# Two mixer stacks with feed-forward layers on one core: spreads by transposition, and another order around the layer norm in the first stack's output stage

## Chip, core and metric

The kernel runs on one core of a Trainium2 chip. The metric is the device time in microseconds of one execution. Before the change the median of three runs is 1272.53 us (1272.1 to 1272.92).

## What is computed

An input of 256 positions by 1024 channels, in float32, goes through two stacks. **Stack 1** is two mixer layers and a final RMS norm; **stack 2** is two layers of feed-forward, mixer, feed-forward, and a last norm. The change touches the mixer layers of stack 1 and the row scale of every norm. Cut to that:

```python
def hybrid_layer(x, ...):                       # stack 1, twice
    h = rmsnorm(x, norm_g)
    proj = h @ w_in                             # 14 pieces of 256 columns in the kernel
    y_a = silu(layernorm(depthwise_conv(a_u * sigmoid(a_v), conv_a_w) + conv_a_b, ln_g, ln_b)) * silu(a_z)
    y_b = b_b * depthwise_conv3(b_c * b_x) * silu(b_z)
    y_c = window_attention(c_q, c_k, c_v, sink) * silu(c_z)
    y_d = neighbourhood_attention(d_q, d_k, d_v, rpb) * silu(d_z)
    return x + concat(y_a, y_b, y_c, y_d) @ w_out
```

The convolution is 31 taps wide. Both attentions have 4 heads of 64 channels and divide by the softmax sum.

## The kernel before, in words

**Precision.** Every large product is made of three: each float32 operand is split into a high part in fp32r, made on ScalarE (`round_hi`, L512), and the remainder, made on VectorE (`split_lo`, L936). TensorE runs high by high, high by low and low by high (`product`, L1659 to L1661). The norm's factor 1/rms is applied after the projection, so TensorE can start before it is known: `spread_rows` (L1724) turns the 128 x 2 values of `rstd` into a row for all partitions, by a plain float32 matmul whose stationary operand is the value broadcast to 128 columns and whose moving operand is the identity; ScalarE copies the result to `row_scale`, by which VectorE's `copy_out` (L989) multiplies each projection on its way out of PSUM. This is done eight times, once for each norm ahead of a projection.

**A mixer layer of stack 1.** Weights arrive in slots of 1 MB through a ring of three. Slots 0 to 13 are the projections in the order of `ORDER_1`, slots 14 to 17 the output matrix in the order `WOUT_1` (c, d, b, a). Every engine has its own hand-written program, a loop over the slots, and semaphores with running counts join them. TensorE's slot i of `project` needs the split weights (`lo_ready`) and a free PSUM bank (`copy_out` of slot i - 2). The attention is done in four units (window attention for the two halves of the queries, then neighbourhood attention for the two). Unit u has its scores after slot u + 7, its softmax on VectorE and ScalarE, its transposition in the midst of slot u + 9 (`turn_probs`, L1800), and its values after slot u + 9 (`values`, L1811), into the PSUM tile `mix`. The exponentials aren't normalized. Instead `finish` on VectorE takes the reciprocal of the four row sums (`row_inv`, 128 x 4, L1016), one slot after the scores, and TensorE's `spread_inverse` (L1820) spreads them over the channels into the PSUM tile `aux`, by four float32 matmuls of 64 columns each, after the values. `gated_y` on VectorE (L1144, L1148) multiplies `aux`, the gate and `mix`; the values of unit u + 1 may be written only after this has read `mix`.

**VectorE's order in a slot** is `copy_out`, `finish`, the softmax's bias and maximum (`soft`, L999, L1004), `gated_y`, some convolution taps (L1129, `DVE_TAPS_AT`), `split_lo`, and a gate product (L1210). The last four taps are in slot 12, behind `gated_y` of the last unit, and then `conv_part` goes up. GpSimd adds the products of the other taps and then the two partial sums (L1582), which raises `conv_ready`.

**The output stage** of stack 1 (slots 14 to 17). Within slot 14 TensorE transposes the convolution to rows of positions (`conv_to_tm`, L1902), VectorE takes mean and variance (L1171, L1172) after `copy_out` of slot 13, GpSimd the inverse root (L1529), VectorE normalizes (L1195), TensorE turns it back within slot 15 (`ln_to_fm`, L1911), VectorE applies gain and bias (L1228), ScalarE makes the tanh of it (L710), and VectorE forms and splits the branch (L1237, L1238, L943, L944). That raises `ya_ready`, for which slot 17 waits; slot 16 waits for the short convolution's branch (`yb_ready`).

Of the kernel before, what the change touches and what calls it, by code (L numbers as in the profile page):

```python
# [11 lines left out]
ACT = mybir.ActivationFunctionType  # L12
# [3 lines left out]
P = 128  # L16
# [65 lines left out]
TURN_AT = 7  # L82
ROT_AT = 4
# [81 lines left out]
def stacks_kernel(nc, a, out):  # L165

    with ExitStack() as ctx:
# [22 lines left out]
        part_sum = sb("part_sum", [P, S])  # L190
        tmp = sb("tmp", [P, 2 * S])
# [120 lines left out]
        ln_ready = sem("ln_ready")  # L312
# [181 lines left out]
        def _(act):  # L494
# [178 lines left out]
            for l in range(DEPTH):  # L673
# [35 lines left out]
                act.wait_ge(ln_ready, l + 1)  # L709
# [207 lines left out]
        def _(dve):  # L917
# [93 lines left out]
            def finish(un, u, has_sink):  # L1011
                c = 4 * (u % 2)
                dve.wait_ge(probs_exp, un + u + 1)
                if has_sink:
                    link(v.tensor_tensor(row_sum[:, c:c + 4], row_sum[:, c:c + 4], sink_e, ALU.add))
                link(v.reciprocal(row_inv[:, c:c + 4], row_sum[:, c:c + 4]))  # L1016
                dve.sem_inc(inv_ready, 1)
# [92 lines left out]
            for l in range(DEPTH):  # L1110
# [43 lines left out]
                for i, name in enumerate(ORDER_1):  # L1154
                    if i == 0:
                        dve.wait_ge(rb_ready, l + 1)
                    if name != "d_v":
                        copy_out(base, i, name, l * NPROJ + i)
                    if i == 4:
                        rotate(step_aux(), proj[:, ix["c_q"], :], cst[:, C_COS:C_COS + S], cst[:, C_SIN:C_SIN + S],  # L1160
                               2, proj[:, ix["c_q"], :])
# [5 lines left out]
                    if i == 13:  # L1167
                        n = step_aux()
                        dve.wait_ge(aux_written, n + 1)
                        for t in range(NT):  # L1170
                            link(v.bn_stats(bn_raw[:, t, :], aux[:, t * S:(t + 1) * S]))  # L1171
                            link(v.bn_aggr(bn[:, t, :], bn_raw[:, t, :]))  # L1172
                        v.tensor_copy(ln_rstd[:], bn[:, :, 1]).then_inc(ho_ready, 1)
# [13 lines left out]
                    if i in DVE_TAPS_AT:  # L1187
                        done = sum(n for at, n in DVE_TAPS_AT.items() if at < i)
                        taps(done, done + DVE_TAPS_AT[i])
                        if done + DVE_TAPS_AT[i] == DVE_TAPS:  # L1190
                            dve.sem_inc(conv_part, 1)
# [8 lines left out]
                    if name in ("a_v", "c_z", "d_z", "b_z", "a_z"):  # L1200
# [24 lines left out]
                n = step_aux()  # L1225
                dve.wait_ge(aux_written, n + 1)
                for c in range(2):
                    ins = v.tensor_scalar(conv_acc[:, c], aux[:, c * S:(c + 1) * S], parA_all[:, l, A_LG + c:A_LG + c + 1],  # L1228
                                          parA_all[:, l, A_LB + c:A_LB + c + 1], ALU.mult, ALU.add)
                    ins.then_inc(aux_read if c else ln_half, 1)  # L1230
                dve.wait_ge(aux_read, n + 2)
                dve.wait_ge(ln_half, l + 1)
                dve.sem_inc(ln_ready, 1)
# [420 lines left out]
        def _(pe):  # L1654
# [64 lines left out]
            def spread_rows(n):  # L1719

                pe.wait_ge(rstd_ready, rms_count(n) * 2 + 2)
                root = rstd_2 if n == DEPTH else rstd
                for t in range(NT):
                    ins = t_.matmul(big[:, 0, t * P:(t + 1) * P], root[:, t:t + 1].to_broadcast([P, P]), ident,  # L1724
                                    start=True, stop=True, skip_group_check=True)
                ins.then_inc(rb_written, 1)
# [88 lines left out]
            def spread_inverse(n, u, order=HORDER):  # L1815
                pe.wait_ge(inv_ready, n + 1)
                for c in range(2):
                    for low in range(2):
                        at = 4 * (u % 2) + order[2 * c + low]
                        ins = t_.matmul(aux[low * HD:(low + 1) * HD, c * P:(c + 1) * P],  # L1820
                                        row_inv[:, at:at + 1].to_broadcast([P, HD]), ident, start=True, stop=True,
                                        skip_group_check=True)
                ins.then_inc(aux_written, 1)
# [15 lines left out]
            for l in range(DEPTH):  # L1839
# [9 lines left out]
                for i, name in enumerate(ORDER_1):  # L1849
                    kind = "TM" if name == "d_v" else "FM"  # L1850

                    def turn_unit():
                        turn_probs(l * 4 + i - SC_1 - 2, i - SC_1 - 2)

                    if i >= 2:
                        between = {TURN_AT: turn_unit} if 0 <= i - SC_1 - 2 < 4 else {}
# [36 lines left out]
                    if 0 <= u - 2 < 4:  # L1893
                        aux_free()
                        spread_inverse(l * 4 + u - 2, u - 2, PLAIN if u - 2 < 2 else HORDER)
                def conv_to_tm():
                    aux_free()
                    pe.wait_ge(conv_ready, l + 1)
                    for t in range(NT):
                        for c in range(2):  # L1900
                            at = t * S + c * P
                            ins = t_.transpose(aux[:, at:at + P], conv_acc[:, c, t * P:(t + 1) * P], ident)  # L1902
                    ins.then_inc(aux_written, 1)

# [9 lines left out]
                for j, grp in enumerate(WOUT_1):  # L1914
# [4 lines left out]
                           {0: {1: conv_to_tm}, 1: {1: ln_to_fm}, 3: {3: lambda: turn_x(l + 1, 0)}}.get(j))  # L1919
# [214 lines left out]
```

## Time and profile before

| | |
|---|---|
| median of three runs | 1272.53 us |
| the profiled execution | 1271.64 us, its span 1269.8 us |
| TensorE matmul busy | 1260.5 us, 99% of the span |
| VectorE busy | 986.7 us, 78% |
| ScalarE busy | 697.5 us, 55% |
| GpSimd busy | 270.0 us, 21% |
| granted TensorE clock over the span | 0.999 of full |

The 1.8 us between the span and the time lie outside of what the profile records. A matmul's recorded duration includes the way through the pipeline, so consecutive ones overlap: the interval between two starts is what one costs, and the busy share can't show short stalls. The chain of waits gives such intervals as its steps. Stack 1 takes the first 257 us, with the two units of layers at 18 to 135 us and 141 to 257 us. Stack 2 is the rest.

### The profile page before, as it was taken

The page shows a single profiled execution, that of the slowest core. Times are in us where ns is not written, and L with a number is a line of the kernel's source. Part 1 is how long each engine was busy: PE and PEld are TensorE (multiplying, and loading weights), DVE is VectorE, ACT ScalarE, POOL GpSimd, SP SyncE. Part 2 cuts the span into 40 slices and gives each one's busy share as a digit, 9 for nine tenths or more (in the row PEclk, how much of TensorE's full clock was granted, in tenths as well). Part 3 has the DMA queues.
Part 4 walks back from the last instruction along what each step waited for, and adds up shares of the span by engine and source line. Part 5 has one row for each costly group of instructions (what it writes and reads, how often), then busy time and mean ns, then how long its engine had stood idle before and what let it go on. Part 6 is the DMA issues. An engine that isn't in the chain of part 4 may idle for free.

```text
span 1269.8 us, 21116 instructions
## 1 busy us (share of the span) xinstructions
PE 1260.5 (99%) x7986; PEld 1124.0 (89%) x7986; DVE 986.7 (78%) x1187; ACT 697.5 (55%) x929; POOL 270.0 (21%) x258
## 2 busy tenths in 40 slices
PE   9999999999999999999999999999999999999998
PEld 8998999888888899988888888888889998888886
DVE  6999789898767679868767778767676986877676
ACT  6674567465444586836444455444458673644444
POOL 2763275283000113201000009100011420100000
PEclk9999999999999999999999999999999999999999
DMA  9854654647666554346666655766654535566661
GB/s 281 257 183 166 202 147 150 180 146 222 198 189 187 156 165 144 128 141 185 196 184 185 198 166 176 214 182 190 198 161 138 166 134 150 177 189 197 193 186 52
DMA packets 281359, 224.02 MB, mean 176 GB/s; under 512 B 25996, under 2 KB 264234, under 8 KB 281288
## 3 DMA queue, kind: packets, MB, share of 16 engines
q1 hardware_dynamic: 279144, 220.23, 57.5%
q10 hardware_dynamic: 2032, 2.67, 0.6%
q8 instruction: 47, 0.77, 0.2%
q14 instruction: 24, 0.20, 0.0%
q0 software_dynamic: 112, 0.15, 0.0%
HBM read 221.85 MB, written 3.14 MB: 177 GB/s over the span
## 4 chain that ended last, share of the span: by engine, by line
PE 90%; DVE 6%; ACT 2%; issue 2%; DMA 0%; POOLq 0%; SPq 0%; DVEq 0%; POOL 0%; ACTq 0%
PE wide L1692 26%; PE wide L1695 13%; PE big L1659 9%; PE big L1660 9%; PE big L1661 8%; PE wide L1659 6%; PE wide L1660 6%; PE wide L1661 6%; DVE w_lo L936 2%; PE wide L1811 1%; PE big L1716 1%; PE big L1800 1%; PE big L1786 1%; DVE work L1345 1%; PE wide L1981 1%
## 5 line engine op out<-in xcount | busy, mean ns | idle before, releaser
L936 DVE TENSOR_TENSOR w_lo<-w_raw,w_hi 128x2048 fp32r<-128x2048 f32 x203 | 475.0, 2342 | 94.5 <-ACT w_hi L512 90.2
L512 ACT ACTIVATE w_hi<-w_raw 128x2048 fp32r<-128x2048 f32 x204 | 389.6, 1911 | 165.0 <-PE big L1661 125.2
L1692 PE MATMUL wide<-h_both,w_hi 128*128 128x512 f32 x1408 | 356.7, 393 | 0.0
L1692 PEld LDWEIGHTS wide<-h_both,w_hi 128*128 128x128 f32 x1408 | 254.6, 189 | 48.5 <-DVE h_both L951 2.0
L1659 PE MATMUL wide<-h_both,w_hi 128*128 128x256 f32 x736 | 213.6, 290 | 0.3 <-DVE h_both L951 0.3
L1660 PE MATMUL wide<-h_both,w_hi 128*128 128x256 f32 x736 | 208.1, 283 | 0.0
L1661 PE MATMUL wide<-h_both,w_lo 128*128 128x256 f32 x736 | 208.1, 283 | 0.0
L1695 PEld LDWEIGHTS wide<-h_both,w_lo 128*128 128x128 f32 x1408 | 194.2, 190 | 15.0
L1695 PE MATMUL wide<-h_both,w_lo 128*128 128x256 f32 x1408 | 198.8, 282 | 0.0
L1659 PE MATMUL big<-w_hi,y_hi 128*128 128x512 f32 x480 | 189.1, 394 | 0.0
L1660 PE MATMUL big<-w_lo,y_hi 128*128 128x512 f32 x480 | 187.3, 390 | 0.0
L1661 PE MATMUL big<-w_hi,y_lo 128*128 128x512 f32 x480 | 187.0, 390 | 0.0
L726 ACT ACTIVATE work<-wide 128x512 f32<-128x512 f32 x88 | 52.5, 597 | 233.9 <-PE wide L1695 233.8
L1659 PEld LDWEIGHTS wide<-h_both,w_hi 128*128 128x128 f32 x736 | 140.8, 191 | 5.3 <-issue 4.4
L1660 PEld LDWEIGHTS wide<-h_both,w_hi 128*128 128x128 f32 x736 | 141.0, 192 | 0.5 <-issue 0.5
L1661 PEld LDWEIGHTS wide<-h_both,w_lo 128*128 128x128 f32 x736 | 140.9, 191 | 0.0
L1528 POOL TENSOR_SCALAR small<-small 128x1 f32<-128x1 f32 (+1 forms) x20 | 4.4, 221 | 599.5 <-ACT probs L516 549.5
L1251 DVE TENSOR_TENSOR work<-wide,work 128x512 f32<-128x512 f32 x88 | 60.7, 689 | 85.0 <-ACT work L726 85.0
L1661 PEld LDWEIGHTS big<-w_hi,y_lo 128*128 128x128 f32 x480 | 90.1, 188 | 19.3
L1659 PEld LDWEIGHTS big<-w_hi,y_hi 128*128 128x128 f32 x480 | 90.3, 188 | 17.0
L1660 PEld LDWEIGHTS big<-w_lo,y_hi 128*128 128x128 f32 x480 | 90.4, 188 | 16.6
L1556 POOL TENSOR_TENSOR work<-work,fz 128x256 f32<-128x256 f32 x60 | 64.6, 1076 | 24.0 <-ACT fz L598 20.2
(254 smaller groups left out, 1459.1 us busy)
## 6 DMA issues: line engine op xcount, KB each, us to landing
w_raw<-in_w_in SPq DMA_DIRECT2D x112, 512.0 KB, 4.7
w_raw<-in_ffn_w_gate SPq DMA_DIRECT2D x88, 512.0 KB, 4.0
w_raw<-in_ffn_w_up SPq DMA_DIRECT2D x88, 512.0 KB, 5.2
w_raw<-in_ffn_w_down SPq DMA_DIRECT2D x88, 512.0 KB, 4.1
w_raw<-in_w_out SPq DMA_DIRECT2D x32, 512.0 KB, 4.3
work<-rpb_shifted SPq DMA_DIRECT2D x32, 64.0 KB, 3.4
rpb_shifted<-rpb_rows SPq DMA_DIRECT2D x10, 147.0 KB
x<-in_x SPq DMA_DIRECT2D x2, 512.0 KB, 6.6
```

Of the source, the lines that this page charges most:

```text
L512: nc.scalar.activation(w_hi[:, r, :], w_raw[:, r, :], ACT.Copy).then_inc(hi_ready, 1)
L726: nc.scalar.activation(tmp_cross[parity].rearrange("p (c s) -> p c s", s=S), wide[:, 2 * parity:2 * parity + 2, S:2 * S], ACT.Copy).then_i ...
L936: v.tensor_tensor(w_lo[:, r, :], w_raw[:, r, :], w_hi[:, r, :].bitcast(F32), ALU.subtract).then_inc(lo_ready, 1)
L1251: v.tensor_tensor(both, wide[:, 2 * parity:2 * parity + 2, 0:S], tmp_cross[parity].rearrange(view, s=S), ALU.add).then_inc(pj_read[parity], 1)
L1345: ins = v.tensor_tensor(packed(queries_of, t, 1), side(qq, t, 1), side(ex, t, 1), ALU.mult)
L1556: g.tensor_tensor(acc, acc, fz[:, n % PROD_RING, :], ALU.add).then_inc(prod_used, 1)
L1659: t_.matmul(o, a_hi, b_hi, start=first, stop=False, skip_group_check=True)
L1660: t_.matmul(o, a_hi, b_lo, start=False, stop=False, skip_group_check=True)
L1661: return t_.matmul(o, a_lo, b_hi, start=False, stop=last, skip_group_check=True)
L1692: t_.matmul(o, hi[:, kt, c], h_both[:, kt].rearrange("p a s -> p (a s)"), start=kt == 0, stop=False, skip_group_check=True)
L1695: ins = t_.matmul(o[:, 0:S], lo[:, kt, c], h_hi[:, kt, :], start=False, stop=kt == KT - 1, skip_group_check=True)
L1716: ins = t_.transpose(big[:, pair, at:at + P], x[:, t, kt * P:(kt + 1) * P], ident)
```

## The change

It has five parts.

- `spread_rows` uses a transposition (`t_.transpose`) of the broadcast values in place of the matmul with the identity, for all eight norms.
- `spread_inverse` uses two transpositions of 128 x 128 in place of four matmuls of 64 columns. For that the values must lie in memory in full width: `finish` writes the reciprocal from a broadcast input into a new tile `inv_wide` (128 x 256 for each unit) and raises `inv_ready` itself. Stack 2 keeps its 128 x 4 reciprocal.
- The last four taps move in slot 12 from behind `gated_y` to right behind `copy_out`; `conv_to_tm` moves from slot 14 into slot 13, ahead of its last of 16 steps; the statistics move ahead of `copy_out` of slot 13.
- The layer norm's gain and bias go from VectorE to ScalarE, as two activations out of PSUM ahead of the tanh.
- The gate product of `a_z` on VectorE goes from slot 13 to behind the split of the short convolution's branch.

```diff
+CONV_AT = 15
+LN_AT = (1, 1)
...
+        inv_wide = sb("inv_wide", [P, 2, NH * HD])
...
                 act.wait_ge(gate_done, l * GATES_1 + GATES_1 + 1)
-                act.wait_ge(ln_ready, l + 1)
+                act.wait_ge(aux_written, l * AUX_1 + AUX_1)
+                for c in range(2):
+                    ins = nc.scalar.activation(conv_acc[:, c], aux[:, c * S:(c + 1) * S], ACT.Identity,
+                                               scale=parA_all[:, l, A_LG + c:A_LG + c + 1],
+                                               bias=parA_all[:, l, A_LB + c:A_LB + c + 1])
+                    ins.then_inc(aux_read if c else ln_half, 1)
+                act.wait_ge(aux_read, l * AUX_1 + AUX_1 + 1)
+                act.wait_ge(ln_half, l + 1)
                 nc.scalar.activation(tanh[:], conv_acc.rearrange("p c w -> p (c w)"), ACT.Tanh,
...
             def finish(un, u, has_sink):
...
-                link(v.reciprocal(row_inv[:, c:c + 4], row_sum[:, c:c + 4]))
-                dve.sem_inc(inv_ready, 1)
+                if un < DEPTH * 4:
...
+                    v.reciprocal(inv_wide[:, u % 2, :].rearrange("p (c low d) -> p c low d", c=2, low=2),
+                                 pairs.unsqueeze(3).to_broadcast([P, 2, 2, HD])).then_inc(inv_ready, 1)
+                else:
+                    v.reciprocal(row_inv[:, c:c + 4], sums).then_inc(inv_ready, 1)
...
+                     if name != "d_v":
                         copy_out(base, i, name, l * NPROJ + i)
+                    if i == 12:
+                        taps(DVE_TAPS - DVE_TAPS_AT[12], DVE_TAPS)
+                        dve.sem_inc(conv_part, 1)
...
-                    if i == 13:
-                        n = step_aux()
-                        dve.wait_ge(aux_written, n + 1)
-                        for t in range(NT):
-                            link(v.bn_stats(bn_raw[:, t, :], aux[:, t * S:(t + 1) * S]))
-                            link(v.bn_aggr(bn[:, t, :], bn_raw[:, t, :]))
-                        v.tensor_copy(ln_rstd[:], bn[:, :, 1]).then_inc(ho_ready, 1)
...
-                    if name in ("a_v", "c_z", "d_z", "b_z", "a_z"):
+                    if name in ("a_v", "c_z", "d_z", "b_z"):
...
                 split_y(y_f[:].rearrange(two, s=S), 2, slice(0, S), yb_ready, l + 1)
-                n = step_aux()
-                dve.wait_ge(aux_written, n + 1)
-                for c in range(2):
-                    ins = v.tensor_scalar(conv_acc[:, c], aux[:, c * S:(c + 1) * S], parA_all[:, l, A_LG + c:A_LG + c + 1],
-                                          parA_all[:, l, A_LB + c:A_LB + c + 1], ALU.mult, ALU.add)
-                    ins.then_inc(aux_read if c else ln_half, 1)
-                dve.wait_ge(aux_read, n + 2)
-                dve.wait_ge(ln_half, l + 1)
-                dve.sem_inc(ln_ready, 1)
+                dve.wait_ge(tanh_ready, l * GATES_1 + GATES_1)
+                v.scalar_tensor_tensor(out=proj[:, ix["a_z"], :], in0=tanh[:], scalar=1.0, in1=proj[:, ix["a_z"], :],
+                                       op0=ALU.add, op1=ALU.mult).then_inc(gate_done, 1)
+                dve.wait_ge(gate_done, l * GATES_1 + GATES_1 + 1)
+                step_aux()
                 split_lo(base, NPROJ + RING)
...
-                    ins = t_.matmul(big[:, 0, t * P:(t + 1) * P], root[:, t:t + 1].to_broadcast([P, P]), ident,
-                                    start=True, stop=True, skip_group_check=True)
+                    ins = t_.transpose(big[:, 0, t * P:(t + 1) * P], root[:, t:t + 1].to_broadcast([P, P]), ident)
...
-            def spread_inverse(n, u, order=HORDER):
+            def spread_inverse(n, u):
                 pe.wait_ge(inv_ready, n + 1)
                 for c in range(2):
-                    for low in range(2):
-                        at = 4 * (u % 2) + order[2 * c + low]
-                        ins = t_.matmul(aux[low * HD:(low + 1) * HD, c * P:(c + 1) * P],
-                                        row_inv[:, at:at + 1].to_broadcast([P, HD]), ident, start=True, stop=True,
-                                        skip_group_check=True)
+                    ins = t_.transpose(aux[:, c * P:(c + 1) * P], inv_wide[:, u % 2, c * P:(c + 1) * P], ident)
                 ins.then_inc(aux_written, 1)
...
-                        between = {TURN_AT: turn_unit} if 0 <= i - SC_1 - 2 < 4 else {}
+                        between = {TURN_AT: turn_unit} if 0 <= i - SC_1 - 2 < 4 else {CONV_AT: conv_to_tm} if i == 13 else {}
...
-                           {0: {1: conv_to_tm}, 1: {1: ln_to_fm}, 3: {3: lambda: turn_x(l + 1, 0)}}.get(j))
+                           {LN_AT[0]: {LN_AT[1]: ln_to_fm}, 3: {3: lambda: turn_x(l + 1, 0)}}.get(j))
```

## Rows read from the trace of the kernel before

**Rows 1.** The page: busy us by engine (share, instructions), and the chain by engine

```profile
PE 1260.5 (99%) x7986; PEld 1124.0 (89%) x7986; DVE 986.7 (78%) x1187; ACT 697.5 (55%) x929; POOL 270.0 (21%) x258
...
PE 90%; DVE 6%; ACT 2%; issue 2%; DMA 0%; POOLq 0%; SPq 0%; DVEq 0%; POOL 0%; ACTq 0%
```

**Rows 2.** Groups of instructions on PE: xcount, busy us, mean ns, idle before

```profile
L1820 PE MATMUL wide<-cst,small 128*64 128x128 f32 x64 | 5.1, 279 | 0.0
L1724 PE MATMUL big<-cst,small 128*128 128x128 f32 x32 | 4.8, 273 | 0.0
```

**Rows 3.** Timeline of PE: start us, us, at a spread of rows

```profile
263.46 0.61 PE L1724 MATMUL big<-cst,small 128*128 128x128 f32 x4
263.82 1.17 PE L1692 MATMUL wide<-h_both,w_hi 128*128 128x512 f32 x4
```

**Rows 4.** The chain of waits, units one and three: start us, step us

```profile
75.16 0.59 PE wide L1820 x8
75.75 0.31 PE wide L1659
78.46 0.87 PE big L1800 x8
...
93.07 0.44 PE wide L1820 x8
```

**Rows 5.** VectorE's small instructions by line: duration ns min/median/max

```profile
L1016 DVE RECIPROCAL small<-small x16: 159/178/180, 69.7 to 1035.4; 128x4 f32<-128x4 f32 x16
...
L1015 DVE TENSOR_TENSOR small<-small x4: 150/152/152, 69.5 to 200.0; 128x4 f32<-128x4 f32 x4
...
L1173 DVE COPY ln_rstd<-bn x2: 169/169/169, 111.6 to 233.7; 128x2 f32<-128x2 f32 x2
```

**Rows 6.** Timeline of VectorE in slots 9 to 11 of layer one

```profile
81.46 0.42 DVE L1148 TENSOR_TENSOR y_f<-wide,tmp 128x256 f32<-128x256 f32 x1
...
86.43 0.17 DVE L1016 RECIPROCAL small<-small 128x4 f32<-128x4 f32 x1
86.85 1.22 DVE L999 SCALAR_TENSOR_TENSOR probs<-big,work 128x1024 f32<-128x1024 f32 x1 [0.25 <-DVE small L1016]
...
89.69 0.42 DVE L1148 TENSOR_TENSOR y_f<-wide,tmp 128x256 f32<-128x256 f32 x1
...
94.11 0.68 DVE L989 TENSOR_TENSOR proj<-wide,row_scale 128x512 f32<-128x512 f32 x1
94.71 0.16 DVE L1016 RECIPROCAL small<-small 128x4 f32<-128x4 f32 x1
```

**Rows 7.** Timeline of PE: the values of units one and two, counted from zero

```profile
82.49 0.33 PE L1811 MATMUL wide<-pT,proj 128*64 128x128 f32 x2
...
91.98 1.09 PE L1811 MATMUL wide<-pT,proj 128*64 128x128 f32 x16
```

**Rows 8.** Timelines of VectorE and GpSimd, slots 12 to 14 of layer one

```profile
100.50 0.68 DVE L989 TENSOR_TENSOR proj<-wide,row_scale 128x512 f32<-128x512 f32 x1
...
103.95 2.05 DVE L1129 SCALAR_TENSOR_TENSOR work<-work,parA_all 128x256 f32<-128x256 f32 x4
106.14 2.29 DVE L936 TENSOR_TENSOR w_lo<-w_raw,w_hi 128x2048 fp32r<-128x2048 f32 x1
...
106.22 2.82 POOL L1582 TENSOR_TENSOR work<-work,part_sum 128x256 f32<-128x256 f32 x1 [2.59 <-DVEq L1191]
```

**Rows 9.** Timelines of VectorE and PE in the output stage of layer one

```profile
108.72 0.39 PE L1661 MATMUL big<-w_hi,y_lo 128*128 128x512 f32 x1
109.18 0.63 PE L1902 MATMUL wide<-cst,work 128*128 128x128 f32 x4
...
125.16 0.39 PE L1659 MATMUL big<-w_hi,y_hi 128*128 128x512 f32 x1
...
118.72 0.99 DVE L1228 TENSOR_SCALAR work<-wide,parA_all 128x256 f32<-128x256 f32 x2
...
124.00 0.69 DVE L944 TENSOR_TENSOR y_lo<-y_f,y_hi 128x512 fp32r<-128x512 f32 x1
```

More of the change, by code:

```diff
@@ L1012, in finish @@
                 c = 4 * (u % 2)
+                sums = row_sum[:, c:c + 4]
                 dve.wait_ge(probs_exp, un + u + 1)
                 if has_sink:
-                    link(v.tensor_tensor(row_sum[:, c:c + 4], row_sum[:, c:c + 4], sink_e, ALU.add))
-                link(v.reciprocal(row_inv[:, c:c + 4], row_sum[:, c:c + 4]))
-                dve.sem_inc(inv_ready, 1)
+                    link(v.tensor_tensor(sums, sums, sink_e, ALU.add))
+                if un < DEPTH * 4:
+                    pairs = sums.rearrange("p (c low) -> p c low", low=2) if u < 2 else sums.rearrange("p (low c) -> p c low", low=2)
+                    v.reciprocal(inv_wide[:, u % 2, :].rearrange("p (c low d) -> p c low d", c=2, low=2),
+                                 pairs.unsqueeze(3).to_broadcast([P, 2, 2, HD])).then_inc(inv_ready, 1)
+                else:
+                    v.reciprocal(row_inv[:, c:c + 4], sums).then_inc(inv_ready, 1)
             def rotate(n, q, cos, sin, width, out):
@@ L1156, in _ @@
                         dve.wait_ge(rb_ready, l + 1)
+                    if i == 13:
+                        n = step_aux()
+                        dve.wait_ge(aux_written, n + 1)
+                        for t in range(NT):
+                            link(v.bn_stats(bn_raw[:, t, :], aux[:, t * S:(t + 1) * S]))
+                            link(v.bn_aggr(bn[:, t, :], bn_raw[:, t, :]))
+                        v.tensor_copy(ln_rstd[:], bn[:, :, 1]).then_inc(ho_ready, 1)
                     if name != "d_v":
                         copy_out(base, i, name, l * NPROJ + i)
+                    if i == 12:
+                        taps(DVE_TAPS - DVE_TAPS_AT[12], DVE_TAPS)
+                        dve.sem_inc(conv_part, 1)
                     if i == 4:
@@ L1186, in _ @@
                         split_lo(base, 6 + RING)
[L1187 removed]
+                    if i in DVE_TAPS_AT and i != 12:
                         done = sum(n for at, n in DVE_TAPS_AT.items() if at < i)
                         taps(done, done + DVE_TAPS_AT[i])
[L1190 to L1191 removed]
                     if i == 13:
@@ L1850, in _, with conv_to_tm @@
                     kind = "TM" if name == "d_v" else "FM"
+                    def conv_to_tm():
+                        aux_free()
+                        pe.wait_ge(conv_ready, l + 1)
+                        for t in range(NT):
+                            for c in range(2):
+                                at = t * S + c * P
+                                ins = t_.transpose(aux[:, at:at + P], conv_acc[:, c, t * P:(t + 1) * P], ident)
+                        ins.then_inc(aux_written, 1)
                     def turn_unit():
@@ L1894, in _ @@
                         aux_free()
[L1895 to L1903, printed above, removed]
+                        spread_inverse(l * 4 + u - 2, u - 2)
                 def ln_to_fm():
```

1 line of the change is left out of this document (removed).

## The prediction, made before the changed kernel ran

> **What bounds the kernel now.** I read the busy shares first and the chain of waits second. TensorE is busy 99% of the span and holds 90% of the chain [rows 1]. But its records overlap, so I took the intervals between starts in the timeline, in stack 1 above all. A spread of rows occupies TensorE from 263.46 to 263.82 us, 0.36 us for four records, and the next matmul starts at once [rows 3]. In the slots of stack 1, starts follow each other without a hole. The one wait that I found there is ahead of `conv_to_tm` in layer one: 0.46 us from the start of the matmul before it, against 0.23 us for a matmul of 512 columns otherwise [rows 9]. So whatever shortens TensorE's own list of work shortens the kernel, and whatever shortens VectorE or ScalarE gives nothing, as long as they stay ahead.
>
> **Spreads of rows.** One float32 matmul leaves two records: 32 for 8 norms by 2 matmuls [rows 2]. A transposition leaves one, and eight of them take 0.87 us in the chain, 0.109 us each [rows 4]; the four records of a spread take the same 0.44 us less the overlap at their end. Two records less at each site are 0.22 us, at eight sites **1.7 us**. ScalarE's copy and VectorE's first `copy_out` wait for this spread, so nothing that follows is held up.
>
> **Spreads of the inverse sums.** Eight units with eight records each make 64 [rows 2]. In the chain a unit costs 0.59 us where it follows scores (units zero and one, with 0.15 us for the change from operands of 64 partitions), and 0.44 us where it follows values of 64 columns [rows 4]. Two transpositions are 0.22 us. The 0.31 us step of the first full matmul behind the spread, against 0.12 us for the next ones [rows 4], is a price for the change of shape; it moves ahead of the transpositions and stays one. So units zero and one save 0.59 - 0.22 = 0.37 us, the others 0.22 us: per layer 1.18 us, for both layers **2.4 us**. In its tensor engine page (TensorE: Matmul & The Clock Gate, Terms) the Trainium skill calls the transposition mode four times faster for float32. The records show a factor of two here; by the page's factor the two spreads together would give 5.7 us, and the time would be 1.6 us lower than mine.
>
> **The wide reciprocal.** It goes on VectorE in slots 8 to 11, where that engine is hardly ever idle. The trace has a reciprocal of four elements only, so I bound it. It took 159 to 180 ns; a two-input operation of four took 150, a copy of two 169 [rows 5]. A floor of 146 ns (150 less four elements of 1.05 ns) and the median of 178 ns give at most 8 ns an element, 2.19 us for 256. One element in 1.05 ns, as in the 0.42 us of a 128 x 256 product [rows 6], gives 0.44 us. The fastest reciprocal allows (159 - 146) / 4 = 3.3 ns, 0.98 us. I take 0.44 us: a copy of two elements takes as long as a reciprocal of four, which leaves nothing for a slow element. Against it stands what goes: the chained wait between the small reciprocal and the softmax, 0.42 us from start to start (86.43 to 86.85) [rows 6]. An unchained operation lets the next start 0.08 us before its end (94.11 + 0.68 against 94.71) [rows 6], so the wide one takes 0.36 us from start to start. VectorE gains 0.06 us a unit: nothing.
>
> **Taps and the turn of the convolution.** The four taps (2.05 us) go from 103.95 us to right behind `copy_out`, which starts at 100.50 us [rows 8]. They end at about 103.2 instead of 106.0 us, and `gated_y` and the weight split come just that much later, with the split again at 106.1 us. GpSimd's sum took 2.82 us because it started at 106.22, 0.08 us behind a split that ran to 108.43 [rows 8]; a product of the same size takes 0.42 us on VectorE. Now it meets short operations at 103.2 us, and I estimate 1.5 us: ready by 104.7 us. TensorE comes to the turn's new place three matmuls ahead of slot 14, at about 107.2 us, and by the savings so far (0.22 + 1.18) at 105.8 us. It doesn't wait. The same four transpositions cost the same there, and the wait of 0.23 us in layer one goes [rows 9]: **0.2 us**.
>
> **The output stage.** The statistics start 1 to 2 us earlier, `copy_out` of slot 13 (0.6 us) falls into the wait for GpSimd's root, VectorE loses the affine step (0.99 us at 118.72) [rows 9], and everything behind comes about 3.5 us earlier: the last split would end at 121.2 us instead of 124.00 + 0.69 = 124.7 us. Slot 17 begins at 125.16 us [rows 9]. That is 0.5 us of room, and TensorE will be there 1.6 us earlier, at 123.5 us. So without this reordering the savings would in part come back as a wait here, and with it there are 2 us of room. The worth of the move is cover. ScalarE's two activations come before a tanh and beside splits; it is busy 55% [rows 1]. It now waits for the gate product of `a_z` before them, at about 116 us, and the weight rounding for slot 18 is queued behind them; TensorE wants that after 130 us. I cost both at nothing. No DMA moves on a queue; their releases come with the splits, which are not later.
>
> **Sum.** 1.7 + 2.4 + 0.2 = 4.3 us. The profiled execution took 1271.64 us, so it becomes 1267.3 us; the median of the runs stands 0.9 us above the profiled one, which makes **1268.2 us**.
>
> **Rival one, a slow reciprocal (slower).** Suppose the wide reciprocal takes 2.19 us, the upper bound. Then each unit adds 2.19 - 0.08 - 0.42 = 1.7 us to VectorE. The point that decides is the room of `gated_y` ahead of the next unit's values. For unit one it is 82.49 - (81.46 + 0.42) = 0.6 us, for unit two 91.98 - (89.69 + 0.42) = 1.9 us [rows 6, 7]; of these the faster TensorE takes 0.4 and 0.7 us. Two reciprocals lie ahead of the first place, three ahead of the second: 3.4 - 0.2 = 3.2 and 5.1 - 1.2 = 3.9 us. The larger is the stall of a layer. The taps come late as well, and I add 0.5 to 1 us for the turn of the convolution. Two layers of about 4.5 us less 4.3 us: +4.6 us, **1277 us**. It decides from about 1.5 us for the reciprocal (stalls of 2.1 us a layer). At the middle value of 0.98 us the stalls sum to about 1 us, 1269 us, which still counts as my forecast. For it speaks the width itself, against it the fastest record. The Trainium skill (VectorE: DVE Perf Modes, First, the fixed hardware budget) speaks against the change here: it has the reciprocal as an iterative divide with a repeat count of 8. If that meant eight cycles for each element, it would be this case; the rows of four elements neither show nor exclude it.
>
> **Rival two, the turn waits (no change).** GpSimd's sum is caught behind a weight split again: that runs from about 105 to 107.3 us, and the sum ends at 107.9 us where TensorE wants it at 105.8. Everything of TensorE is queued behind the turn, so 2.1 us are lost in each layer: 4.3 - 4.2, **1272 us**. For it: before, the sum was caught in just that way [rows 8]. Against it: it would have to start 1.9 us later than I reckon.
>
> **Rival three, no gain from transposing.** A broadcast or wide operand costs as much in transposition as in the matmul, or the change of shape is paid twice. Only the 0.2 us and perhaps the spreads of rows stay: **1271 us**.
>
> **How the numbers follow.** A measurement of this kernel tells about 0.2% from no change, 2.5 us: faster is below 1270.0, slower above 1275.1 us. My forecast has 0.60, the slow reciprocal 0.22 (of it 0.14 above 1275, 0.05 within, 0.03 below 1270), the turn 0.10, no gain 0.08 (one quarter of it below 1270). Faster: 0.60 + 0.03 + 0.02 = 0.65; within: 0.05 + 0.10 + 0.06 = 0.21; slower: 0.14. The range runs from 1267.0 (a quarter more than the sum) to 1275.0 and leaves out the far part of rival one and a little below.
>
> **What would show it.** On TensorE: 16 records of one-pass spreads of rows in place of 32, and 16 in place of 64 for the sums; 0.22 us steps in the chain; no start late at the values of units one and two, nor at the turn. On VectorE: a reciprocal of 128 x 256 at about 0.44 us. If it shows 1.5 us or more, or the values start behind `gated_y`, the forecast is wrong. If GpSimd's sum ends after 106 us, rival two holds. Busy time falls on VectorE by 1 us or so and rises on ScalarE by 2 us, without worth.

## The result, and the profile after

The changed kernel takes 1277.56 us in the median of seven runs (1275.99 to 1278.1), against 1272.53 us before: a ratio of 1.0038 (95% interval 1.0026 to 1.0049), 5.0 us slower. The forecast was 1268.2 us. Of the page of the changed kernel, what answers to [rows 1]:

```profile
span 1276.0 us, 20974 instructions
...
PE 1259.7 (99%) x7922; PEld 1123.7 (88%) x7922; DVE 998.2 (78%) x1183; ACT 699.7 (55%) x933; POOL 251.8 (20%) x258
```

TensorE has 64 instructions less, as reckoned (16 and 48), and VectorE is busy 11.5 us longer where I had expected a little less. The group that does it, instructions by line on VectorE (busy us, mean ns, idle before):

```profile
L1028 DVE RECIPROCAL inv_wide<-small 128x256 f32<-128x256 f32 x8 | 14.0, 1746 | 0.1
L1031 DVE RECIPROCAL small<-small 128x4 f32<-128x4 f32 x8 | 1.4, 175 | 6.1 <-ACT probs L574 6.1
```

The wide reciprocal takes **1746 ns**, four times the 440 ns that I took and well over the 980 ns which I had derived from the fastest small one [rows 5]. The waits of TensorE (in total, times, longest) say what it costs:

```profile
PE wide L1864 <- POOL work L1593: 4.1, 2, 2.1
PE wide L1821 <- DVE y_f L1162: 3.0, 2, 1.6
...
PE wide L1917 <- DVE proj L1210: 0.6, 1, 0.6
```

L1864 is the turn of the convolution, waiting for GpSimd's sum, L1821 are the values of the next unit, waiting for `gated_y`, L1917 is the turn back. None of these three waits was listed before. VectorE and GpSimd around the turn in layer one, in the timeline, to be read against [rows 8]:

```profile
106.88 0.68 DVE L998 TENSOR_TENSOR proj<-wide,row_scale 128x512 f32<-128x512 f32 x1
107.48 2.04 DVE L1143 SCALAR_TENSOR_TENSOR work<-work,parA_all 128x256 f32<-128x256 f32 x4
...
109.75 0.72 POOL L1593 TENSOR_TENSOR work<-work,part_sum 128x256 f32<-128x256 f32 x1 [5.92 <-DVEq L1182]
```

`copy_out` of slot 12 starts at 106.88 us, 6.4 us later than before. Of this 1.4 us is the later start of the whole layer (the table below), and the other 5.0 us is what four units at 1.25 us make. The taps follow at 107.48 us, where the prediction had them at about 101 us, and GpSimd, which had been idle for 5.9 us, adds its sums at once. TensorE had issued its last matmul ahead of the turn at 108.27 us. So the reordering worked as meant (the sum isn't caught behind a weight split any more: 0.72 us against 2.82), but what it waits for came too late.

**Where the time went, by landmarks.** The start of the spread of rows marks a stage's end on TensorE. From the timelines of PE (us; the last column is from the third spread to the last matmul, which starts at 1263.19 us before and at 1269.29 us after):

| kernel | first spread at | layer one | layer two | stack 2 |
|---|---|---|---|---|
| before | 18.65 | 122.46 | 122.35 | 999.73 |
| changed | 20.02 | 125.08 | 126.29 | 997.90 |
| difference | +1.37 | +2.62 | +3.94 | -1.83 |

The sum is 6.1 us, the difference between the two last matmuls; the spans differ by 6.2 us. The first column is not the change's: the first eight transpositions of the input took 1.94 us in the changed kernel's profile and 1.07 us before, and among the kernels below the first spread comes at 18.5 to 18.9 us or at 19.8 to 20.1 us with no relation to what they contain. The medians over runs differ by 5.0 us, and the other three columns together by 4.7 us. The waits and the slow stretch described next account for it: 7.7 us of waits and 1.5 us of slow clock are lost, and the savings come to about 4.5 us.

In layer two there is more than waits. TensorE around the turn, timeline (the wait in brackets), and the granted clock in stretches (columns: stretch, its length, busy us and instructions of PE, PEld, DVE, ACT and POOL, PEclk, DMA share, GB/s):

```profile
235.98 1.07 PE L1864 MATMUL wide<-cst,work 128*128 128x128 f32 x4 [2.07 <-POOL work L1593]
...
238.35 0.63 PE L1672 MATMUL big<-w_hi,y_lo 128*128 128x512 f32 x1
238.77 0.63 PE L1670 MATMUL big<-w_hi,y_hi 128*128 128x512 f32 x1
...
239.76 0.39 PE L1670 MATMUL big<-w_hi,y_hi 128*128 128x512 f32 x1
239.99 0.40 PE L1671 MATMUL big<-w_lo,y_hi 128*128 128x512 f32 x1
```

```profile
230.00:233.60 3.60, 3.60 (x32) 3.60 (x31) 3.53 (x5) 0.63 (x1) 0.00 (x0) 1.00 0.02 7
233.60:235.90 2.30, 0.31 (x3) 0.11 (x1) 2.03 (x5) 0.00 (x0) 0.79 (x2) 1.00 0.85 322
...
238.20:239.20 1.00, 1.00 (x3) 0.71 (x3) 1.00 (x1) 1.00 (x1) 0.00 (x0) 0.50 0.00 0
239.20:240.00 0.80, 0.80 (x5) 0.68 (x4) 0.80 (x2) 0.51 (x1) 0.00 (x0) 0.86 0.04 10
```

TensorE stood idle for 2.07 us, and behind it the granted clock is 0.50, 1.2 GHz, for 3.4 us, until about 239.4 us. The interval of a matmul of 512 columns is 0.42 us there instead of 0.23 us. The five intervals from 237.49 to 239.54 us lose 0.9 us and the shorter ones ahead of them 0.6 us: the wait costs its length and 1.5 us more. In layer one, behind a wait of the same length, the clock stayed at 1.00.

### The profile page after: what moved, and what is told of

It is laid out like the page before. It is cut to its first block, busy times and chain, and to the rows that moved or that the text cites. A ratio compares the mean times of both kernels' runs of the same rounds, so it can differ in the third digit from the quotient of the medians.

```text
span 1276.0 us, 20974 instructions
## 1 busy us (share of the span) xinstructions
PE 1259.7 (99%) x7922; PEld 1123.7 (88%) x7922; DVE 998.2 (78%) x1183; ACT 699.7 (55%) x933; POOL 251.8 (20%) x258
## 4 chain that ended last, share of the span: by engine, by line
PE 90%; DVE 7%; issue 2%; DMA 0%; POOL 0%; ACT 0%; POOLq 0%; SPq 0%; DVEq 0%
PE wide L1703 25%; PE wide L1706 13%; PE big L1670 8%; PE big L1671 8%; PE big L1672 8%; PE wide L1670 7%; PE wide L1671 7%; PE wide L1672 7%; DVE w_lo L945 2%; PE big L1727 1%; PE wide L1987 1%; DVE probs L1008 1%; PE big L1796 1%; DVE work L1143 1%; DVE inv_wide L1028 1%
## 5 line engine op out<-in xcount | busy, mean ns | idle before, releaser
L1567 POOL TENSOR_TENSOR work<-work,fz 128x256 f32<-128x256 f32 x60 | 61.3, 1021 | 27.8 <-ACT fz L600 24.0
```

Source lines behind the costliest of these rows:

```text
L1567: g.tensor_tensor(acc, acc, fz[:, n % PROD_RING, :], ALU.add).then_inc(prod_used, 1)
```

## The experiments

Theory R: the wide reciprocal makes VectorE late, everything else is worth what the prediction says. Rivals: theory O (the new order costs by itself) and theory T (transposing saves nothing). `widths` ran once; all others ran four to eleven times, beside runs of the kernel before, against which their ratios stand. The expectations and the last table call the kernels by name: in the order of the experiments `copy_new_order`, `rows_only`, `order_only`, `spreads_old_order`, `copy_old_order`, `ballast`, `widths`, `turn_back`, `reciprocal_late`, `copy_late`, `copy_late_ln3` and `unchained`. The chain of which experiment 12 speaks, and `link` in the code, are waits of VectorE for its own last operation.

**1. The same, with a quick way to the wide operand.** Only the softmax units of stack 1 differ from the changed kernel:

```diff
+                    link(v.reciprocal(row_inv[:, c:c + 4], sums))
+                    inv = row_inv[:, c:c + 4]
...
-                    v.reciprocal(inv_wide[:, u % 2, :].rearrange("p (c low d) -> p c low d", c=2, low=2),
+                    v.tensor_copy(inv_wide[:, u % 2, :].rearrange("p (c low d) -> p c low d", c=2, low=2),
```

> The changed kernel with one edit: the reciprocal is taken of the four sums again (128 x 4, chained), and a copy spreads it to 128 x 256. Theory R (the reciprocal's 1.75 us delays VectorE): a unit then costs about 0.17 + 0.05 + 0.35 us against 1.75 us, the waits of TensorE at the values and at the convolution's turn (7.7 us in the trace) go, and the 4.3 us of the two spreads remain: 1268.0 to 1269.2 us. Theory O (the new order costs by itself: the turn in slot 13 comes before its sum): a wait of about 2 us a layer at the turn stays, 1272 us or more. Theory T (the transpositions save nothing): 1272 to 1273 us without a wait.

Measured: **1268.94 us**, ratio 0.9975 (0.9965 to 0.9985). The wide operand is now a copy:

```profile
L1030 DVE COPY inv_wide<-small 128x256 f32<-128x256 f32 x8 | 3.0, 376 | 0.3
L1027 DVE RECIPROCAL small<-small 128x4 f32<-128x4 f32 x8 | 1.4, 170 | 0.1
```

One substitution turns 5.0 us lost into 3.0 us gained. Theory R holds, O and T fall. Two kinds of wait remain here, 1.0 us at the values of unit one in layer one and 0.7 us a layer at the turn back.

**2. The spread of rows alone**, in the kernel before:

```diff
-                    ins = t_.matmul(big[:, 0, t * P:(t + 1) * P], root[:, t:t + 1].to_broadcast([P, P]), ident,
-                                    start=True, stop=True, skip_group_check=True)
+                    ins = t_.transpose(big[:, 0, t * P:(t + 1) * P], root[:, t:t + 1].to_broadcast([P, P]), ident)
```

> The kernel before with the spread of rows by transposition alone. Theory R and my sum: two records less at eight sites, 0.22 us each, -1.7 us, 1270.8 us. Theory T: no difference, 1272.5 us.

Measured: 1270.17 us against 1271.95 us of its round, ratio 0.9987 (0.9978 to 0.9996): -1.8 us against -1.7 expected. By the landmarks (the table behind experiment 12) it is 1.7 us: 0.22, 0.24 and 1.24. The row of the third spread has become

```profile
264.46 0.38 PE L1724 MATMUL big<-cst,small 128*128 128x128 f32 x2
```

two records for four [rows 3]. Theory T falls for this part by itself.

**3. The new order alone**, with both spreads as before. Against the changed kernel, next to the two lines of experiment 2 turned back:

```diff
-                    ins = t_.transpose(aux[:, c * P:(c + 1) * P], inv_wide[:, u % 2, c * P:(c + 1) * P], ident)
+                    for low in range(2):
+                        at = 4 * (u % 2) + order[2 * c + low]
+                        ins = t_.matmul(aux[low * HD:(low + 1) * HD, c * P:(c + 1) * P],
+                                        row_inv[:, at:at + 1].to_broadcast([P, HD]), ident, start=True, stop=True,
+                                        skip_group_check=True)
```

> The changed kernel with both spreads as before (plain matmuls, small reciprocal): what is left is the new order and the affine step on ScalarE. Theory R: no wait at the turn, the one of 0.23 us in layer one gone, 1272.3 us (-0.2). Theory O: about 2 us a layer, 1276 to 1277 us.

Measured: 1271.6 us against 1271.95 us, ratio 0.9998 (0.9989 to 1.0007). The interval holds the expected 0.2 us and zero. TensorE waits neither at the turn nor behind it in this trace, so the affine step on ScalarE, the gate behind the split and the earlier turn cost nothing. Theory O falls.

**4. Both spreads with the wide reciprocal, in the old order.** The kernel before with the change's `spread_rows`, `finish` and `spread_inverse`, the last of them:

```diff
+                    ins = t_.transpose(aux[:, c * P:(c + 1) * P], inv_wide[:, u % 2, c * P:(c + 1) * P], ident)
```

> The kernel before with both spreads by transposition and the wide reciprocal, in the old order. Theory R: VectorE is 5 us late by slot 12 (four units of 1.25 us), the taps stand behind the last unit as before, so TensorE waits at the values as in the changed kernel (1.6 us a layer), for the sum at the turn in slot 14 about 3 us a layer, and perhaps at slot 17: 1277 to 1280 us, no faster than the changed kernel. Theory O: without the new order it is faster than the changed kernel by 4 us, 1273 us.

Measured: 1283.76 us, ratio 1.0092 (1.0076 to 1.0107), 6 us over the changed kernel and above my range. Its waits on TensorE:

```profile
PE wide L1903 <- POOL work L1588: 8.2, 2, 4.1
PE wide L1816 <- DVE y_f L1154: 3.9, 2, 2.2
```

The old order leaves the turn twice the wait (4.1 us a layer). The half clock comes in both layers, for 3.4 us in layer one (114.1 to 117.5 us) and for 6.8 us in layer two (240.4 to 247.2 us), of which TensorE was idle until 242.3 us. My range had 9.2 us of waits and nothing for the clock. There were 12.1 us of waits, 4.3 us more than in the changed kernel, and the clock took 4.2 us, 2.7 us more than there (my estimate, half of the slow stretches in which TensorE worked). So the new order is cover, and worth much more beside a late VectorE than alone, though more than a third of the difference is the clock and not the wait.

**5. The quick way in the old order.** As experiment 4, with experiment 1's `finish`:

```diff
+                    v.tensor_copy(inv_wide[:, u % 2, :].rearrange("p (c low d) -> p c low d", c=2, low=2),
```

> The kernel before with both spreads by transposition, the wide operand by the small reciprocal and a copy, in the old order. If the new order is the cover that I said it is, TensorE, by 1.6 us earlier, now waits at the turn of the convolution in slot 14 (1 to 1.5 us a layer, VectorE's taps being late by 1.2 us too) and at slot 17: 1270 to 1272 us, slower than the same in the new order (1268.9). If the order is worth nothing: 1268 to 1269 us.

Measured: 1270.86 us, ratio 0.9989 (0.9980 to 0.9998), 1.9 us behind the same in the new order (by the landmarks of the two layers 2.7 us). The trace has 1.7 us a layer of waiting for GpSimd's sum at the turn, and 0.7 us once for a weight split; at slot 17, where I had expected a wait too, there is none. The order that is worth nothing by itself (experiment 3) is worth 2 to 3 us as soon as TensorE gets there earlier.

**6. The reciprocal as ballast.** In the kernel before, behind each small reciprocal of stack 1:

```diff
+                if un < DEPTH * 4:
+                    v.reciprocal(inv_wide[:, u % 2, :].rearrange("p (h d) -> p h d", h=4),
+                                 row_sum[:, c:c + 4].unsqueeze(2).to_broadcast([P, 4, HD]))
```

> The kernel before, and behind each of the eight small reciprocals of stack 1 a second one of 128 x 256 whose result nobody reads. Theory R: VectorE gets 1.67 us more a unit (1.75 less 0.08), more than in the changed kernel (1.25), with the old order. By the room at the values, 0.6 us with two and 1.9 us with three of them ahead in layer one (0.7 and 2.0 us in layer two), TensorE waits about 3.1 us there in each layer, then at the turn of the convolution in slot 14 for the sum behind late taps, 3 us or more: 1283 to 1286 us. If a late VectorE did not matter: 1272 us.

Measured: 1285.76 us, ratio 1.0104 (1.0089 to 1.0119). The waits are 1.5 us a layer at the values and 3.5 us at the turn:

```profile
PE wide L1906 <- POOL work L1586: 7.1, 2, 3.5
PE wide L1815 <- DVE y_f L1152: 3.0, 2, 1.5
```

The total came out as expected, by another division: the values wait half as long as I had reckoned, and layer one has a stretch at half clock (116.7 to 120.1 us) that I had not reckoned at all. Layer two has none, behind an equal wait of 3.5 us. A reciprocal that nobody reads costs 13 us by the medians, 12 us by the landmarks of the two layers: the loss of the changed kernel needs nothing of the spreads.

**7. Four sizes of it**, units zero to three with 16, 64, 128 and 256 elements:

```diff
+                    n = (4, 16, 32, 64)[u]
+                    v.reciprocal(inv_wide[:, u % 2, 0:4 * n].rearrange("p (h d) -> p h d", h=4),
+                                 row_sum[:, c:c + 4].unsqueeze(2).to_broadcast([P, 4, n]))
```

> The kernel before with a second, unread reciprocal of 128 x 16, 64, 128 and 256 behind the small ones of units zero to three. Theory: a floor of about 150 ns and 6.2 ns an element, so 0.25, 0.55, 0.95 and 1.75 us. If a reading with step zero were the slow thing and not the division, the four sizes would not lie on one line with the 0.175 us of four plain elements.

```profile
L1021 DVE RECIPROCAL inv_wide<-small 128x256 f32<-128x256 f32 x2 | 3.5, 1752 | 0.3
L1017 DVE RECIPROCAL small<-small 128x4 f32<-128x4 f32 x16 | 2.8, 174 | 6.2 <-ACT probs L573 6.1
L1021 DVE RECIPROCAL inv_wide<-small 128x128 f32<-128x128 f32 x2 | 1.9, 954 | 0.3 <-DVE small L1017 0.2
L1021 DVE RECIPROCAL inv_wide<-small 128x64 f32<-128x64 f32 x2 | 1.1, 553 | 0.3
L1021 DVE RECIPROCAL inv_wide<-small 128x16 f32<-128x16 f32 x2 | 0.5, 254 | 0.3
```

(1752 - 254) / 240 = **6.24 ns an element**, on a floor of 154 ns; the small one by this line is 179 ns and has 174. The broadcast reading isn't what is slow: a copy of the same width with the same broadcast took 0.38 us on average (0.29 us in most cases, experiment 1). The four plain elements lie near the same line, but with a scatter of 159 to 180 ns they prove little by themselves, and a wide reciprocal of plain elements was not run.

**8. The turn of the convolution back in slot 14**, the wide reciprocal kept, the turn back half a slot later:

```diff
-LN_AT = (1, 1)
+LN_AT = (1, 3)
...
-                        between = {TURN_AT: turn_unit} if 0 <= i - SC_1 - 2 < 4 else {CONV_AT: conv_to_tm} if i == 13 else {}
+                        between = {TURN_AT: turn_unit} if 0 <= i - SC_1 - 2 < 4 else {}
...
-                           {LN_AT[0]: {LN_AT[1]: ln_to_fm}, 3: {3: lambda: turn_x(l + 1, 0)}}.get(j))
+                           {0: {1: conv_to_tm}, LN_AT[0]: {LN_AT[1]: ln_to_fm}, 3: {3: lambda: turn_x(l + 1, 0)}}.get(j))
```

> The changed kernel, wide reciprocal and all, but with the turn of the convolution in slot 14 again, 1.8 us of TensorE's work later, and the turn back half a slot later. Theory R: the waits at the values stay (1.5 us a layer), the one at the turn of 2.1 us a layer shrinks to some 0.3 us, the one at the turn back goes, and with the long wait goes the stretch at half clock behind it: 5 to 6 us less than the changed kernel, 1271.5 to 1273 us. If the turn's place did not matter: 1277 us.

Measured: 1277.29 us, ratio 1.0041 (1.0027 to 1.0055), the same as the changed kernel. **My expectation was wrong by 5 us.** The wait at the turn did go, and came back elsewhere:

```profile
PE wide L1821 <- DVE y_f L1162: 3.9, 2, 2.3
PE big L1670 <- DVE y_lo L953: 1.8, 1, 1.8
...
PE wide L1908 <- POOL work L1593: 0.3, 1, 0.3
```

1.8 us at a slot of the output matrix in layer two, for a branch that VectorE splits (L953), and 0.8 us more at the values. TensorE's waits for the other engines in the two layers come to 6.4 us, against 7.7 us in the changed kernel. The rest is the clock. I had expected the half clock to go, and it is there twice (columns as above):

```profile
85.30:88.60 3.30, 3.30 (x24) 2.50 (x21) 3.27 (x4) 3.30 (x7) 0.02 (x1) 0.51 0.00 0
249.00:252.00 3.00, 3.00 (x9) 2.33 (x8) 2.93 (x4) 2.61 (x3) 0.00 (x0) 0.50 0.66 164
```

The first stands behind the wait of 2.26 us at the values, the second behind the 1.82 us in layer two; each lasts 3.4 us, in which TensorE does 1.7 us less. Layer one takes 125.2 us, layer two 126.7 us, near the changed kernel's 125.1 and 126.3 us. So VectorE's list, still late, was paid for at other places, in part by waits and in part by a slower TensorE. The equal total is not proof that a wait comes back in full: without the second slow stretch, behind which no wait follows in its layer, it could have been 1.7 us lower.

**9. The wide reciprocal behind `gated_y`.** As in experiment 10, but the reciprocal itself stands there, in a function called behind `gated_y`:

```diff
+            def widen(u):
...
+                v.reciprocal(inv_wide[:, u % 2, :].rearrange("p (c low d) -> p c low d", c=2, low=2),
+                              pairs.unsqueeze(3).to_broadcast([P, 2, 2, HD])).then_inc(inv_ready, 1)
```

> As copy_late, but with the wide reciprocal itself behind gated_y instead of the copy. VectorE's list is as long as in the changed kernel; only the softmax and gated_y of a slot no longer stand behind the reciprocal of their own slot. Theory L (the sum of VectorE's work sets the time, and a wait moved away comes back later): 1276 to 1278 us, with the waits at the values smaller and those at the turn and behind as large. Theory P (its place ahead of the softmax is what costs): 1270 to 1272 us.

Measured: 1275.23 us, ratio 1.0024 (1.0014 to 1.0034), between the two ranges, nearer to theory L (the sum) than to theory P (the place). Four spreads now wait for the reciprocal, the waits at the turn are much shorter than theory L had them (1.1 us in all against 4.1 us), no wait is longer than 1.1 us, and the clock stays full:

```profile
PE wide L1833 <- DVE inv_wide L1033: 3.8, 4, 1.1
...
PE wide L1922 <- DVE proj L1215: 1.3, 2, 0.7
PE wide L1869 <- POOL work L1598: 1.1, 2, 0.6
```

Together TensorE waits 6.7 us in the two layers against 7.7 us, and the 1.5 us of slow clock are gone. The two layers are 2.2 us shorter than in the changed kernel, which this explains within 0.4 us. So moving the reciprocal took away about 1 us of waits, and 6.7 us stayed with a list of the same length.

**10. The copy behind `gated_y`**, small reciprocal where it was:

```diff
                     if 0 <= u - 2 < 4:
                         gated_y(u - 2, 4 if u - 2 < 2 else 6)
+                    if 0 <= u - 1 < 4:
+                        widen(u - 1)
```

> As copy_new_order, but the copy stands behind gated_y instead of ahead of the softmax. Theory: the wait of 1.0 us at the values of unit one in layer one goes, and those for the normalized values (0.7 us a layer) stay since TensorE is earlier by what it gains: 1267.9 to 1268.9 us.

Measured: **1268.03 us**, ratio 0.9966 (0.9954 to 0.9978). The total is as expected, the waits are the other way round: those at the turn back are gone, and the 1.0 us at unit one's values in layer one stays. Its cause stays open. In this trace ScalarE begins to round a slot's weights at 37.76 us, after 4.9 us of waiting for the DMA, against 36.42 us before. But in experiment 3 it begins at 37.77 us too, and TensorE doesn't wait there: `gated_y` of unit one ends 0.6 us later than before, and here 1.5 us later. All four kernels with the copy have this wait, 1.0 us each time.

**11. And the turn back half a slot later:**

```diff
-LN_AT = (1, 1)
+LN_AT = (1, 3)
```

> As copy_late, and the turn back of the normalized values comes half a slot (2.7 us) later, at the fourth quarter of slot 15. Theory: its waits of 0.7 to 0.8 us a layer go, slot 17 still finds its branch ready: 1.5 us less than copy_late, 1266.5 to 1267.5 us. If the branch is too late for slot 17, as much comes back there.

Measured: 1267.68 us, ratio 0.9962 (0.9948 to 0.9975). Against experiment 10 that is no difference that these runs can tell: the waits it was made to remove weren't there any more.

**12. The stack 2 part of the change.** I had not priced that `finish` there drops the chained wait and the separate increment. In the kernel before, only that:

```diff
+                else:
+                    v.reciprocal(row_inv[:, c:c + 4], row_sum[:, c:c + 4]).then_inc(inv_ready, 1)
```

> The kernel before, and only in stack 2 the reciprocal raises the semaphore itself, with no chained wait and no separate increment (the changed kernel does so too, which I had taken for nothing). In the traces of the kernels that have this, each of stack 2's two mixers takes 0.3 us less than in rows_only. Theory: VectorE sets the pace there, so this is its doing: -0.5 to -0.6 us in the trace from the third spread of rows to the end, 1271.9 us. If it is something else of the change: no difference in that stretch.

Measured: 1271.65 us against 1272.01 us, ratio 0.9994 (0.9984 to 1.0003), not told apart by the runs. In the traces the stretch from the third spread to the last matmul is 999.22 us against 999.73 us, and the two mixers of stack 2 take 134.30 and 134.24 us against 134.56 and 134.51 us: 0.26 and 0.27 us, which is the whole of it. That VectorE sets the pace in these mixers fits this, and no run tests it by itself.

The landmarks of all, in us:

| kernel | layer one | layer two | stack 2 | median |
|---|---|---|---|---|
| rows_only | 122.24 | 122.11 | 998.49 | 1270.17 |
| order_only | 122.35 | 122.37 | 999.77 | 1271.6 |
| unchained | 122.47 | 122.35 | 999.22 | 1271.65 |
| copy_old_order | 124.55 | 122.67 | 997.97 | 1270.86 |
| copy_new_order | 122.72 | 121.82 | 997.96 | 1268.94 |
| copy_late | 122.28 | 120.74 | 997.98 | 1268.03 |
| copy_late_ln3 | 121.85 | 120.75 | 997.90 | 1267.68 |
| reciprocal_late | 124.69 | 124.47 | 997.95 | 1275.23 |
| turn_back | 125.18 | 126.70 | 997.92 | 1277.29 |
| spreads_old_order | 128.96 | 129.10 | 997.99 | 1283.76 |
| ballast | 129.05 | 127.65 | 999.81 | 1285.76 |
| widths | 127.37 | 127.59 | 999.75 | 1281.9 (one run) |

## Why the prediction was wrong, point by point

**The failed step is the term for the wide reciprocal.** I took 0.44 us, at one element in 1.05 ns. It measured 1.75 us, 6.24 ns an element. The bounds were right (0.44 to 2.19 us); the choice between them was not. I read a rate out of the difference between two operations of four elements, where a rate of 6.24 ns makes 21 ns and the scatter of the same instruction is 159 to 180 ns [rows 5]. From such rows no value in the range can be preferred, least of all by their minimum, whose 3.3 ns an element became a supposed ceiling. The median, 178 ns, gives (178 - 154) / 4 = 6 ns with the floor measured now. The Trainium skill (VectorE: DVE Perf Modes, First, the fixed hardware budget) has the reciprocal as an iterative divide with a repeat count of 8, and I had weighed that lower than the copy of two elements at 169 ns. The widths agree with it in that an element costs several times what a copy's does. The figure itself, 6.24 ns, is this case's measurement; I can't derive it from the 8.

**Rival one is what happened**, with its place, sign and size: 1277 us foreseen, 1277.6 measured, for a reciprocal of 2.19 us. Part of that agreement is luck. With 1.75 us a unit costs 1.25 us more, not 1.7 us. By my working the stall of a layer would be 3 x 1.25 - 1.2 = 2.6 us at the values of unit two; TensorE waited 1.6 us at those of unit one instead, and 2.1 us at the turn, where I had put 0.5 to 1 us. The half clock in layer two (1.5 us) wasn't in the working at all. Taking the largest single stall was the weak point. Experiments 8 and 9 point to a better rule: VectorE's lateness at the end of its list, here 4 x 1.25 = 5.0 us a layer less its slack, is lost at whatever places TensorE meets it. The slack was not measured apart; what TensorE waited was 4.1 and 3.7 us a layer in the changed kernel and 3.4 and 3.3 us in experiment 9, and the half clock, which came and went, adds to that.

**The spreads of rows**: 1.7 us predicted, 1.8 us measured (experiment 2). Right.

**The spreads of the inverse sums and the sum of 4.3 us**: hidden by the waits in the changed kernel, but to be read where the reciprocal is out of the way. The timelines of PE at unit one of layer one, before and then in experiment 10, from the start of the scores to the second matmul behind the spread:

```profile
83.52 1.13 PE L1786 MATMUL big<-proj 64*128 64x256 f32 x8
84.58 0.66 PE L1820 MATMUL wide<-cst,small 128*64 128x128 f32 x8
...
85.39 0.28 PE L1660 MATMUL wide<-h_both,w_hi 128*128 128x256 f32 x1
```

```profile
84.54 1.13 PE L1803 MATMUL big<-proj 64*128 64x256 f32 x8
85.60 0.44 PE L1835 MATMUL wide<-cst,inv_wide 128*128 128x128 f32 x2
...
86.00 0.28 PE L1678 MATMUL wide<-h_both,w_hi 128*128 128x256 f32 x1
```

That is 1.87 us against 1.46 us, 0.41 us saved where 0.37 was predicted. In the same way unit two, from the start of the values, takes 1.68 us against 1.43 us, 0.25 us saved where 0.22 was predicted. With units zero (0.41 us) and three (0.26 us) a layer saves 1.3 us, both 2.7 us against 2.4 us in the sum, and layer two of experiment 10, where no wait is left, agrees: it is 1.6 us shorter than before, 0.24 us of it by the spread of rows. The medians agree: experiments 10 and 11 have 4.4 and 4.8 us less than before, of which 0.5 us is experiment 12's, and by the landmarks, with that 0.5 us in them, it is 3.5 and 4.0 us with a wait of 1.0 us still in layer one. So these terms were right within what can be told. By the factor of four in the Trainium skill (TensorE: Matmul & The Clock Gate, Terms) the two spreads together would save 5.9 us, as an estimate (the 5.7 us of the prediction was 0.2 short by the same working); the records and these times agree with the factor of two.

**The turn of the convolution**: the sum without the weight split over it was foreseen at 1.5 us and took 0.72 us; the wait of 0.2 us gone is too small for these runs (experiment 3). That it would be ready in time hung on the reciprocal and failed with it.

**The output stage as cover**: right. The same kernels with the old order are slower by 1.9 us with the quick way and by 6.2 us with the slow one, of this about 2.7 us by the clock (experiments 5 and 4). ScalarE's two activations took 1.02 us together and nobody waited for them or for the tanh behind them.

**"Stack 2 keeps its reciprocal"**: an edit that I read over. It is worth 0.5 us in the traces, too little for the runs to tell.

## What to carry to other kernels

A wide operand for a transposition is cheap if it is copied (0.29 us for 128 x 256) and dear if it is divided (1.75 us): take the reciprocal of the few values and spread the result, not the other way round. An operation whose cost for each element isn't in the trace should not be priced from a handful of elements, because a factor of six in the rate hides in 20 ns; if it stands on an engine that is busy all through a stage, the forecast hangs on that one number and should be split accordingly. And when an engine runs without a gap beside the one that bounds, count how late its whole list becomes, not how long it stalls the other at one place: in experiments 8 and 9 most of a wait that was moved away came back at the next place.

## What the runs showed that I had not expected

- The float32 reciprocal on VectorE takes 154 ns and 6.24 ns for each element of a partition, on one line from 16 to 256 elements, with the input broadcast.
- Behind a wait of 2.07 us the granted clock was 0.50 for 3.4 us (236.0 to 239.4 us) and a matmul of 512 columns took 0.42 us instead of 0.23 us. In the layers of all these kernels it came behind waits of 1.82, 2.07, 2.26, 3.39, 3.41, 3.54 and, twice, 4.09 us, and it did not come behind others of 1.7, 2.07, 2.25 and 3.53 us. So it is no fixed price of a wait, and what decides stays open. Such a stretch cost 1.5 to 1.7 us more, an estimate from half of its length, once (behind 4.09 us, where it lasted 6.8 us) about 2.5 us.
- The first transpositions of the input, ahead of anything that was edited, ran at about half the rate in some profiles, and the first spread came up to 1.7 us later. The granted clock was 1.00 in both cases, so the clock isn't the reason. A comparison of two single traces takes this along, so I compared stretches between landmarks. The median of the kernel before itself lay anywhere from 1271.78 to 1272.53 us in the five sets of runs, so differences below about 0.7 us between medians of different sets tell nothing.
